# A hybrid decoder step on one core: the first gate one weight piece later, and the carried state decayed where it is placed

## The reference

```
proj = h @ w_in                                  # 2048 columns in, split into the branches
xl   = causal_conv(xl, ...)                      # 4 taps, recurrent group, 1024 channels
r, i = sigmoid(xl @ w_a + b_a), sigmoid(xl @ w_i + b_i)   # the two gates, blocks of 64
a    = exp(-8 r softplus(-lambda)); b = sqrt(1 - a^2) * i * xl
h_t  = a_t h_(t-1) + b_t ;  out_l = h * gelu(gl)
# the other group (SSD), 2 chunks of 128 tokens, 16 heads of 64 x 128 state
states[c]   = B^T (decay_last * x dt)            # the chunk's contribution
h_in[1]     = states[0] ;  h_T = d[1] * states[0] + states[1]
y = (C B^T * L) (x dt) + C h_in exp(cumsum)      # within the chunk, and from the state
```

## Time and profile before

| | us |
|---|---|
| median of 3 runs (lowest, highest) | 2186.86 (2186.82, 2187.64) |
| the profiled execution's own time | 2185.31 |
| its span in the profile | 2183.6 |
| mean granted TensorE clock over the span | 0.992 |
| VectorE, ScalarE, GpSimd busy | 1209.0, 856.8, 123.5 |

### The profile page before, as it was taken

The page is one execution under the profiler, slowest core; times in us unless marked ns, Lnnn a source line. Parts: engine busy times, 40 slices in busy tenths (PEclk is TensorE's granted clock), DMA queues, the critical chain, the costliest instruction groups (busy, mean ns, idle before and its releaser), DMA issues.

```text
span 2183.6 us, 39972 instructions
## 1 busy us (share of the span) xinstructions
PE 2122.1 (97%) x17405; PEld 1979.4 (91%) x17405; DVE 1209.0 (55%) x1664; ACT 856.8 (39%) x1050; POOL 123.5 (6%) x146
## 2 busy tenths in 40 slices
PE   6999999999999999989988999999999999999998
PEld 4988889988888889989888998999999999999998
DVE  4355576444444445577788977444444444445565
ACT  3433333333333333356545534333333333333332
POOL 0000000000000000011675000000000000000000
PEclk9999999999999999999999999999999999999999
DMA  9988887799888877756554575774677886745453
GB/s 357 341 299 295 281 284 249 268 348 357 306 308 310 309 279 245 247 154 204 160 163 142 174 258 200 272 251 155 227 243 247 307 281 239 251 162 175 147 173 118
DMA packets 394269, 534.17 MB, mean 245 GB/s; under 512 B 13031, under 2 KB 357999, under 8 KB 375407
## 3 DMA queue, kind: packets, MB, share of 16 engines
q1 hardware_dynamic: 371792, 519.28, 69.1%
q10 hardware_dynamic: 22303, 12.33, 2.0%
HBM read 524.37 MB, written 7.19 MB: 243 GB/s over the span
## 4 chain that ended last, share of the span: by engine, by line
PE 87%; DVE 8%; ACT 2%; issue 1%; DMA 1%; SPq 1%; ACTq 0%; DVEq 0%
PE main L1637 23%; PE main L1638 23%; PE main L1639 23%; PE b L1560 5%; PE main L1703 4%; PE main L1705 3%; PE main L1704 3%; DVE w_lo L994 3%; ACT w_hi L683 1%; PE b L1570 1%; SPq L530 1%; PE b L1583 1%; DMA first<-in_w_ada 1%; DVE ntile L1087 1%; DVE h_lo L1092 1%
## 5 line engine op out<-in xcount | busy, mean ns | idle before, releaser
L994 DVE TENSOR_TENSOR w_lo<-raw,w_hi 128x1024 fp32r<-128x1024 f32 (+2 forms) x720 | 795.2, 1112 | 871.0 <-ACT w_hi L683 869.7
L683 ACT ACTIVATE w_hi<-raw 128x1024 fp32r<-128x1024 f32 (+2 forms) x720 | 685.0, 956 | 1065.2 <-PE main L1639 902.7
L1637 PE MATMUL main<-h_hi,w_hi 128*128 128x264 f32 x2960 | 853.4, 288 | 12.8 <-DVE w_lo L994 4.5
L1638 PE MATMUL main<-h_lo,w_hi 128*128 128x264 f32 x2960 | 845.7, 286 | 0.0
L1639 PE MATMUL main<-h_hi,w_lo 128*128 128x264 f32 x2960 | 844.3, 285 | 0.0
L1637 PEld LDWEIGHTS main<-h_hi,w_hi 128*128 128x128 f32 x2960 | 561.5, 190 | 33.5 <-DVE w_lo L994 23.5
L1638 PEld LDWEIGHTS main<-h_lo,w_hi 128*128 128x128 f32 x2960 | 559.9, 189 | 0.5
L1639 PEld LDWEIGHTS main<-h_hi,w_lo 128*128 128x128 f32 x2960 | 559.7, 189 | 0.0
L1637 PE MATMUL main<-act_hi,w_hi 128*128 128x264 f32 x1408 | 402.1, 286 | 0.0
L1639 PE MATMUL main<-act_hi,w_lo 128*128 128x264 f32 x1408 | 400.4, 284 | 0.0
L1638 PE MATMUL main<-act_lo,w_hi 128*128 128x264 f32 x1408 | 399.8, 284 | 0.0
(11 more groups left out here) (271 smaller groups left out, 989.7 us busy)
## 6 DMA issues: line engine op xcount, KB each, us to landing
raw<-in_w_up SPq DMA_DIRECT2D x132, 1024.0 KB, 5.2
ada<-in_w_ada SPq DMA_DIRECT2D x112, 1024.0 KB, 8.6
raw<-in_w_down SPq DMA_DIRECT2D x96, 768.0 KB, 5.1
raw<-in_w_up SPq DMA_DIRECT2D x88, 512.0 KB, 5.3
raw<-in_w_in SPq DMA_DIRECT2D x36, 1024.0 KB, 5.3
ada<-in_w_ada_f SPq DMA_DIRECT2D x32, 1024.0 KB, 10.2
ada<-in_w_ada SPq DMA_DIRECT2D x56, 512.0 KB, 7.7
raw<-in_w_down SPq DMA_DIRECT2D x32, 512.0 KB, 4.4
```

The source lines that it names most:

```text
L683: A(split_view(w_hi, m, kind), raw_piece(m, kind), ACT.Copy).then_inc(hi_done, 1)
L994: TT(split_view(w_lo, m, kind), raw_piece(m, kind), split_view(w_hi, m, kind).bitcast(F32), ALU.subtract).then_inc(lo_done, 1)
L1637: MM(out, wh, hi[:, k, :], start=k == 0, stop=False)
L1638: MM(out, wh, lo[:, k, :], start=False, stop=False)
```

## The change

Three edits. TensorE's gates of the first tile of a recurrent step (`gates(2t)`) are issued inside part 3, between pieces 6 and 7, and no longer after part 2's other tasks. ScalarE's `gate_tanh(2t)` moves from part 2 to part 3, ahead of `gate_tanh(2t + 1)`. VectorE's multiplication of `s0` by the decay is issued at the end of part 4's item work, behind `item_m` and ahead of the recurrence's products, and no longer in part 14; there a wait on VectorE's own chain stands in its place.

```diff
@@ ScalarE, act_tasks
                 if kind == "lru":
                     if j == 1:
                         conv_first(6 + t)
-                    if j >= 2:
-                        gate_tanh(2 * t + j - 2)
                     if j == 3:
+                        gate_tanh(2 * t)
+                        gate_tanh(2 * t + 1)
                         act.wait_ge(gate_taken, 4 * (t + 1))
@@ VectorE, dve_tasks
+                    if r == 4:
+                        dve.wait_ge(st_placed, 4)
+                        s0_decayed.append(ch.add(TT(s0[:, :, :], s0[:, :, :], cdf[:, :].unsqueeze(2).to_broadcast([P, KW, P]), ALU.mult)))
                     if r == 14:
 
                         dve.wait_ge(st_made, 3)
-                        dve.wait_ge(st_placed, 4)
-                        ch.link(TT(s0[:, :, :], s0[:, :, :], cdf[:, :].unsqueeze(2).to_broadcast([P, KW, P]), ALU.mult))
+                        ch.wait(s0_decayed[0])
                         TT(s0[:, 0:4, :], s0[:, 0:4, :], b5[:, :].rearrange("p (t n) -> p t n", n=P), ALU.add)
@@ TensorE, pe_tasks and the loop over pieces
                     if j < 2:
                         col_rows(2 * t + j)
-                    else:
-                        gates(2 * t + j - 2)
+                    if j == 3:
+                        gates(2 * t + 1)
...
+                                if kind == "lru" and m == 6:
+                                    gates(2 * what)
```

More of the change, by code:

```diff
@@ L1275, in sum_item @@
                 dve.tensor_reduce(samp[:, 4 * g + i, 4 * half:4 * half + 4], prod[n % 2], AX_X, ALU.add).then_inc(st_sum, 1)
+            s0_decayed = []
             def dve_tasks(kind, t, j, s, o_, e_):
```

## The result

| | before | after |
|---|---|---|
| median (lowest to highest, runs), us | 2185.17 (2183.91–2187.64, 7) | 2194.89 (2192.9–2197.86, 7) |
| the profiled execution's own time, its span | 2185.31, 2183.6 | 2197.5, 2195.8 |
| granted clock over the span | 0.992 | 0.989 |

The account below looks back on a forecast made before the run. The prediction took a VectorE–ScalarE loop as the bound in the recurrent steps, TensorE only following. Shifts 0.3 + 2.2 + 1.9 − 1.8 = +2.6 us, less 1.05 slack, gave +1.5: 2188.4 us, range 2184.0 to 2191.0.

Parts of the forecast that it names:

- Gates one piece later, 0: First tile's gates behind weight piece 6: TensorE's wait only changes its name; priced at nothing, bounds 0 and −7.6 us.
- sign (1): Gates at 1090 and 1128 stop waiting for cval; the next piece's first matmul waits for w_lo, some 2 us each.
- Rival one: TensorE is the limit: 7.6 us of gate waits and 1 to 2 us at lower clock go; −9, 2178; 5%.
- Its tanh in part 3, +2.5 us: Two activations add 0.72 us to each step's path in part 3: 0.3 first step, 2.2 others; bounds 1.1 and 2.9.
- Sign (2): Four tanh in a row on ScalarE, and VectorE's step-start waits for w_hi longer by about 0.7 us.
- Multiply in part 4, +1.9, and −1.8 in part 14: Moved multiply and scans beside GpSimd cost 1.9 us (1.2 to 3.3); part 14 gets back 1.8 (1.15 to 2.31).
- sign (3): Multiply of s near 1077 takes 1.2 us, and the scans behind it over 2 us the pair.
- The slack of 1.05 us and TensorE's place behind it: Near y_item(10) TensorE can absorb 1.05 us of VectorE's delay; after 1204 the rest passes on one for one.
- sign (5): TensorE newly waits for w_lo or dmat between 1190 and 1205, with y_item(10) at about 1205.1.
- Sign (4): Broadcast's wait at 1177.90 gone or under 1 us, and granted clock at 1.00 from about 1181 on.
- four: Multiply pushes scans and part 5's splits under GpSimd, tanh costs 0.72 in all steps: +4.0 to +5, 2191.9; 8%.
- Rival two: Only the last step counts, waits for GpSimd's products swallow earlier delays: shift −1.6 or less, about 2184; 12%.

Follow-up runs that it names:

- x3: Kernel before with only the first tile's gate matmuls one weight piece later, tanh still in part 2; 0.9999 of the kernel before.
- x1: Kernel before with only the multiply of s0 moved from part 14 to part 4; 0.9985 of the kernel before.
- x4: Changed kernel with the first tile's tanh in part 3 ahead of the DMA issues and exponential; 0.9985 of the kernel before.
- x10: Changed kernel with the old order of gates and tanh in the last recurrent step only; 1.0016 of the kernel before.
- x12b: Kernel before with the second tile's two tanh made twice in each recurrent step, order of gates and banks unchanged; 1.0003 of the kernel before.
- x14: Kernel before with an added multiply of s0 by one in part 4, the true multiply still in part 14; 0.9991 of the kernel before.
- x8: Kernel before with the multiply of s0 by the decay left out; 0.999 of the kernel before.
- x11: Kernel before with the multiply of s0 moved to the end of part 3's VectorE work, ahead of the w_hi wait; 0.9981 of the kernel before.

## Why the prediction failed, step by step

The side was right, slower, and from the right one of the three edits; the size was not, and the reason is a wait that the sum does not have.

*That the end is set by VectorE and ScalarE, and TensorE only follows:* for the gates' place in the kernel before, x3 bears it out. But it was argued from VectorE's waits alone. ScalarE, the other half of the loop, waited for TensorE before the change as well: from 1030 to 1260 it waited 8.4 us once for the gates, and 11.3 us in ten times for the pieces that free the buffers of `w_hi`. In the changed kernel the statement is untrue, because the change itself put TensorE into the ring.

*Gates one piece later, 0:* right. −0.2 us alone (interval −2.0 to +1.7), and in x3 the wait changed its name as sign (1) said, at 1.42 and 1.65 us instead of 2. Rival one, that these 7.6 us are to be had, is out.

*Its tanh in part 3, +2.5 us: this is the step that failed.* The prediction said of it that two activations "leave part 2, where the splits that follow do not wait for `w_hi`, so nothing is gained there", and "0.72 us is added to the path in each step". It priced what the tanh takes and looked only at what waits behind it on ScalarE. It did not ask who waits for its result on another engine: TensorE, for the two banks. Measured alone +11.8 us against bounds of 1.1 to 2.9. Sign (2), four tanh in a row, was wrong in just this way: there are two pairs with TensorE's gates and 2.28 us of idle time between them, and the waits for `w_hi` grew by 2.1, 3.2, 0.7 and 1.3 us. The wait stood in the code of `gates`, and the order on ScalarE showed that the tanh was now behind the exponential, which before waits for VectorE each time.

*Multiply in part 4, +1.9, and −1.8 in part 14:* the mechanism at its place was right, sign (3) to the digit: 1.22 us and 3.02 us for the scans, and the split of part 8 1.4 us later in x1. The sum was wrong: −3.3 us by the ratio, because in the step from part 8 to part 12 VectorE's same instructions took 3.8 us less, 2.5 of it where three of them missed GpSimd's large passes, and part 14 and what is around it gave 1.0. No term of the sum stood for that step. The rule of the Trainium skill, SBUF — State Buffer, Who interferes with whom, that the later of the two waits for the other's whole instruction, fits these rows again: the one multiply of 128x1024 took 1.22 us with GpSimd idle and 2.31 beside its passes.

*The slack of 1.05 us and TensorE's place behind it:* the mechanism was right, its size some 0.75 us by the offsets, and x1, x4 and x10 show the wait for `w_lo` that sign (5) meant, 0.88, 0.87 and 0.82 us. In the changed kernel it did not decide. Sign (4) was half right: the broadcast at 1183.67 waits no more, but the clock was granted at 0.73 from 1181 to 1193 and 0.80 from there to 1202, as TensorE stood 8.86 us in between. Sign (5) was wrong for the changed kernel: no waits from the gates to `y_item(10)`, which counted from the transposes came 8.0 us late and not 1.5, since TensorE arrived late itself.

*The rivals:* four had the right side, from mishaps of VectorE and GpSimd that were not the cause. None named the banks. Rival two's sum is wrong in itself: it subtracts the slack from a shift of −1.6 us, but where VectorE comes earlier there is no slack to use up.

What stays open: how VectorE's share of the tanh's 11.8 us comes about step by step. x4 takes away TensorE's wait for the banks and ScalarE's wait for the gates at once, and so does not part them. The clean test gives the second tile's gates banks of their own; it was not made. x12b bounds what the two activations cost by their time alone (at most 2.6 us).

## What to carry to other kernels

Before an instruction is moved later, list who waits for it on every engine, and not only for the value it writes but for the buffer it frees by reading: a bank used twice in a step makes its first reader part of the second writer's path. Then look at the instruction it is now queued behind, and what that one waits for. Where there is room, put it ahead of that wait and not behind it. And where VectorE and GpSimd both work through a step, an edit of 1.2 us shifts which of their instructions meet, which was worth 4 us here; so the bounds of such an edit should let it gain as well as cost.

## What the runs showed of the hardware

That adding a pass of 1.22 us to VectorE left the kernel no slower (x14, 0.9991) was not expected; nor was it that leaving one of 2.31 us out gave less than moving it (x8 and x11, −2.2 and −4.2 us; the intervals overlap, but `y_item(10)` comes 2.9 and 5.2 us earlier). A pass of this size takes 1.22 us with GpSimd idle and 2.31 or 2.06 beside it; here are the two in x14, and then the one in x11, which VectorE's wait for `w_hi` behind it hides (1.52 us instead of 2.94):

```profile
1080.92 1.22 DVE L1359 TENSOR_TENSOR s<-s,ones 128x1024 f32<-128x1024 f32 x1
...
1176.42 2.31 DVE L1364 TENSOR_TENSOR s<-s,cdf 128x1024 f32<-128x1024 f32 x1
```

```profile
1068.00 2.06 DVE L1394 TENSOR_TENSOR s<-s,cdf 128x1024 f32<-128x1024 f32 x1
...
1071.57 4.05 DVE L994 TENSOR_TENSOR w_lo<-raw,w_hi 128x1024 fp32r<-128x1024 f32 x2 [1.52 <-ACT w_hi L683]
```

And TensorE's long waits cost a second time: the gates' pair takes 1.22 us in the changed kernel after it has stood 5.32, 7.22 or 8.86 us, at a granted clock of 0.50, and 0.68 us with no wait (1097.07, the first tile's of the second step), at 1.00, so the one at 1.2 and the other at 2.4 GHz. The length of the one wait does not settle it: a pair takes 1.22 us after 1.68 us in the earlier trace rows (1180.26, behind another wait of 1.83 at 1177.90), and 0.69 after 3.53 in x3 (1141.62, above). The row with no wait:

```profile
1097.07 0.68 PE L1804 MATMUL b<-cval,gates_w 128*128 128x264 f32 x2
```
